# Who makes the high half of a weight tile: a cast DMA, or a copy on GpSimd

## The chip, the cores and the metric

One core of a Trainium2 chip runs the whole program. The metric is the device time of one execution in microseconds, the median of several runs. Times inside an execution come from one profiled execution, counted from the start of its span.

## What is computed

Three transformer layers on a sequence of 512 tokens of width 1024. The first two are the same layer with two sets of weights:

```
mod  = silu(c) @ ada_w + ada_b                      # six vectors of 1024
h    = rms_norm(x) * (1 + sc_m) + sh_m
proj = h @ w_in                                     # inputs of three attentions, three gates
x    = x + g_m * ((sum over NA, MLA, GQA of sigmoid(gate) * (o @ w_br)) @ w_out)
h    = rms_norm(x) * (1 + sc_f) + sh_f
x    = x + g_f * ((silu(h @ w_gate) * (h @ w_up)) @ w_down)
```

NA is a neighbourhood attention, GQA and MLA are dense ones. The third layer mixes a short convolution, a linear recurrence (RG-LRU) and an RWKV-7 recurrence in chunks, merges them with gates, and ends with an MLP of width 4096. All is float32. Each matrix product of a weight is made of three passes on TensorE over rounded numbers (type fp32r): with w = w_hi + w_lo and h = h_hi + h_lo it sums w_hi h_hi + w_hi h_lo + w_lo h_hi.

## The kernel before

**Weight stream.** All weights pass through two rings of four slots. `raw` holds tiles of 128 x 1024 float32 as they lie in HBM (512 KB; some are 128, 256, 384 or 512 columns wide). `wR` holds for each tile the high half, `wR[:, u, 0]`, which is the weight rounded to fp32r, and the low half, `wR[:, u, 1]`, which is raw minus high, rounded too. There are 468 tiles (`G_USED`), 145 for each of the first two layers. A tile of 1024 columns feeds 24 matmuls (8 steps of 128 rows, three passes each), one of 256 or 512 columns 6 or 12.

**Raw ring.** It is shared with the rows of `ada_w`: the list `RAW` mixes 96 "mod" entries with the tiles. A mod entry is not for TensorE: VectorE multiplies it with silu(c) and sums (L1428), which frees the slot (`ada_used`). 16 mod entries come first, the other 80 lie between the tiles of layer 0: one for each attention step, three for each of the 8 MLA steps, one for each pair of tiles behind them, one for each pair in the gate/up product. Layer 1 and the third layer have none. SyncE walks through `RAW` in order (L493 to L508): before entry r it waits until entry r - 4 is done with, a tile by `tile_ready` (its subtraction has ended), a mod entry by `ada_used`.

**GpSimd (POOL).** It has nothing else to do than the loop of L515 to L532. `cast(g)` (L515) waits for the raw tile and for a free slot of `wR` (`tile_used`, counted by TensorE's last matmul on a tile), and issues a DMA from `raw` to `wR[:, u, 0]` that rounds on its way (L522). The loop issues `cast(g + 1)` first (`AHEAD = 1`), then waits for `hi_ready` of tile g and subtracts (L531), which counts `tile_ready`. So the subtraction of tile g stands in the queue behind the two waits of the cast of tile g + 1.

**TensorE.** `need_tile` waits for `tile_ready`; the passes are L327 to L329. In the first two layers the dense products are cut into steps and filled between the parts of 32 attention steps: scores (L1015), turning the probabilities (L1025), times V (L1035). Steps 0 to 7 are NA, 8 to 23 GQA, 24 to 31 MLA; a step of MLA holds 12 dense steps (a gate tile with 8, a branch tile of 512 columns with 4). Behind step 31 the rest of the gates and MLA branches follows: pairs of a 1024 and a 256 column tile, 10 dense steps. Then come the output product (`mg`), gate/up and down (`act_f`).

**VectorE (DVE)** works in program order. In an MLA step it makes the maxima, the probabilities (`prob`, L1660), mod entries, and merges a branch (L1524, L1528). In the third layer, for each of 8 blocks m of 128 channels, TensorE waits at L1162 for `kkB`, which ends a chain of VectorE work: `kB` (L1835), the end of the block before (`finish`, L1852 to L1868), `vB`, four scans (L1889), `kkB`, `aB`, `kB` (L1897 to L1906). I call this stretch, where block m follows block m - 1, a change of block.

Of the kernel before, what the change touches and what calls it, by code (L numbers as in the profile page):

```python
# [22 lines left out]
NMOD = 6  # L23
EPS = 1e-6
RING = 4
AHEAD = 1


T_IN, T_MLA, T_MERGE, T_OUT, T_GU, T_DOWN = 0, 16, 20, 20 + 4 * KD, 20 + 5 * KD, 20 + 5 * KD + 2 * KF
# [137 lines left out]
G_USED = G_MLP + 64  # L167
# [49 lines left out]
RAW_AT = {what: r for r, what in enumerate(RAW)}  # L217


def ring_source(g):  # L220

    if g >= G_OUT2:
        return T_OUT2 + g - G_OUT2, 0, 1024
    if g >= G_B2:
        return MIX_SLOTS[g - G_B2]
    l, n = divmod(g, G_LAYER)
    if n >= G_OUT:
        return T_LAYER * l + T_OUT + n - G_OUT, 0, 1024
    tile, col, cols = SLOTS[n]
    return T_LAYER * l + tile, col, cols  # L230
# [101 lines left out]
def build(nc, x, c, weights, ada_b, vec1, rpb, vec2_in, vecx_in, tables1, out):  # L332
    dram_bias = nc.dram_tensor("bias_rows", (DEPTH * 4 * 15, 127), F32, kind="Internal")
    dram_toeplitz = nc.dram_tensor("bias_toeplitz", (DEPTH * 4, GRID, 15, SKEW), F32, kind="Internal")
    with ExitStack() as ctx:
        def sb(name, shape, dt=F32, into=None):
            return (into or ctx).enter_context(nc.sbuf_tensor(name, shape, dt))

        def sem(name):
            return ctx.enter_context(nc.semaphore(name))  # L340
# [6 lines left out]
        raw = sb("raw", [P, RING, 1024])  # L347
        wR = sb("wR", [P, RING, 2, 1024], F32R)
# [48 lines left out]
        passed = sem("passed")  # L397
# [42 lines left out]
        s_pad = sem("s_pad")  # L440
        s_bias = sem("s_bias")
        raw_ready = [sem(f"raw_ready{i}") for i in range(RING)]
        hi_ready = [sem(f"hi_ready{i}") for i in range(RING)]
        tile_ready = sem("tile_ready")
        tile_used = sem("tile_used")
        ada_used = sem("ada_used")
# [44 lines left out]
        @block.sync  # L491
        def _(sp):
            sp.dma_start(cs[:], c.broadcast_to([P, D])).then_inc(s_c, 16)  # L493
            for r, (what, n) in enumerate(RAW):
                if r == RING:
                    for dst, src in ((xT, x), (adab, ada_b), (vl, vec1), (tab, tables1["axial"]), (vecx, vecx_in),
                                     (tabm, tables1["rope"]), (colmask, tables1["colmask"]), (ident, tables1["ident"]),
                                     (blk, tables1["blk"])):
                        sp.dma_start(dst[:], src).then_inc(s_in, 16)
                if r >= RING:  # L500
                    before, number = RAW[r - RING]
                    if before == "mod":
                        sp.wait_ge(ada_used, number + 1)
                    else:
                        sp.wait_ge(tile_ready, number + 1)
                tile, col, cols = (n, 0, 1024) if what == "mod" else ring_source(n)
                source = weights[tile if what == "mod" else N_ADA + tile, :, col:col + cols]
                sp.dma_start(raw[:, r % RING, 0:cols], source).then_inc(raw_ready[r % RING], 16)  # L508
            sp.wait_ge(fin_ready, KD)
            sp.dma_start(out, xT[:]).then_inc(s_out, 16)  # L510
            sp.wait_ge(s_out, 16)

        @block.gpsimd
        def _(pool):

            def cast(g):
                u, cols, r = g % RING, ring_source(g)[2], RAW_AT["tile", g]
                pool.wait_ge(raw_ready[r % RING], (r // RING + 1) * 16)
                if g >= RING:
                    pool.wait_ge(tile_used, g - RING + 1)  # L520
                pool.sem_inc(passed, 1)
                pool.dma_start(wR[:, u, 0, 0:cols], raw[:, r % RING, 0:cols]).then_inc(hi_ready[u], 16)  # L522

            for g in range(AHEAD):
                cast(g)
            for g in range(G_USED):
                if g + AHEAD < G_USED:
                    cast(g + AHEAD)
                u, cols, r = g % RING, ring_source(g)[2], RAW_AT["tile", g]
                pool.wait_ge(hi_ready[u], (g // RING + 1) * 16)  # L530
                nc.gpsimd.tensor_tensor(wR[:, u, 1, 0:cols], raw[:, r % RING, 0:cols], wR[:, u, 0, 0:cols], ALU.subtract  # L531
                                        ).then_inc(tile_ready, 1)  # L532

        @block.scalar
        def _(act):
# [54 lines left out]
            for l in range(DEPTH):  # L590
# [19 lines left out]
                def turn(j):  # L610
                    _, tile, _ = TURNS[j]
                    act.wait_ge(vt_turned, 5 * l + j + 1)
                    if 32 * l + 8 * (j // 3) > 0:
                        act.wait_ge(pv_done, 32 * l + 8 * (j // 3))
                    A(vt[:, tile].rearrange("p a n -> p (a n)"), ps[:, PT + j % 2, :], ACT.Copy).then_inc(vt_copied, 1)
# [231 lines left out]
        def _(pe):  # L847
# [72 lines left out]
            for l in range(DEPTH):  # L920
# [7 lines left out]
                def dense(first, end):  # L928

                    for p in range(first, end):  # L930
                        kind, n, _, slot, last = PRODS[p]
                        t, signal = TI + slot, tile_used if last else part_ready
                        if kind == "in":
# [29 lines left out]
                def turn(j):  # L963
                    _, _, tile = TURNS[j]
                    evacuated(pe, Count(PR + {4: 0, 5: 1, 15: PIDX["in", 15], 8: PIDX["v", 0], 16: PIDX["v", 1]}[tile]))
                    before = 64 * l + {0: 0, 1: 0, 2: 8, 3: 40, 4: 40}[j]
                    if before:
                        pe.wait_ge(p_copied, before)
                    for b in range(4):
                        mm = nc.tensor.transpose(ps[:, PT + j % 2, b * P:(b + 1) * P], pj[:, tile, b * P:(b + 1) * P], ident[:])  # L970
                    mm.then_inc(vt_turned, 1)
# [1239 lines left out]
```

## Time and profile before

| | |
|---|---|
| median of 3 runs | 3166.22 us (3163.53 to 3168.85) |
| the profiled execution's own time | 3169.7 us |
| its span | 3167.9 us |
| TensorE busy | 2930.3 us, 92% |
| VectorE busy | 1698.2 us, 54% |
| GpSimd busy | 1279.5 us, 40% |
| of it: 468 subtractions, L531 | 1016.2 us |
| of it: 468 cast DMA instructions, L522 | 267.4 us |
| cast DMA traffic | 218.4 MB of 503.85 MB, 19.5% of the 16 DMA engines' time |
| mean granted clock of TensorE | 0.973 |

A row of the profile by line names the source line, the engine, the operation, what it writes and reads, its shape, how often it ran, its busy time and mean, and then how long its engine sat idle just before it and what ended that. In a timeline each row is an instruction, or several that were merged (x3): start, duration, then in brackets an idle time of that engine and what ended it. The chain of waits goes back from the last instruction, at each step to what released it. A row of VectorE can be longer than its work: time in which an instruction is held up after it has started counts as busy.

### The profile page before, as it was taken

What the parts mean: (1) busy time and instruction counts of PE and PEld (TensorE: products, weight loads), DVE (VectorE), ACT (ScalarE), POOL (GpSimd) and SP (SyncE); (2) the same over time, 40 slices, a digit from 0 to 9 for tenths busy, and PEclk for the clock granted to TensorE, in tenths of its full rate; (3) what the DMA queues carried; (4) which work ended last, traced back from release to release, by engine and by line L of the source; (5) the groups of instructions that cost most, each with busy time, mean ns of one, the idle gap of its engine ahead of it and who ended that gap; (6) DMA issues with size and microseconds to landing.
All of it is one profiled execution on the core that took longest, in us unless ns stands there. A gap on an engine that the chain in (4) does not pass through costs nothing.

```text
span 3167.9 us, 44134 instructions
## 1 busy us (share of the span) xinstructions
PE 2930.3 (92%) x18104; PEld 2265.4 (72%) x18104; DVE 1698.2 (54%) x2263; ACT 698.0 (22%) x1183; POOL 1279.5 (40%) x940
## 2 busy tenths in 40 slices
PE   2899988999998999999999969999999999999997
PEld 1666666787786767777888757777777777778786
DVE  4488775566513776445443274665465466463352
ACT  2343220200002443201000033223233323220000
POOL 1323334455564333354555522333233323345553
PEclk8899999999999999999999989999999999999999
DMA  8644556577766233364555532333233333445553
GB/s 271 180 136 141 190 200 200 178 239 236 235 218 176 93 93 122 120 199 162 193 192 197 198 109 99 106 119 121 89 125 114 112 104 117 142 159 190 182 192 113
DMA packets 174631, 503.85 MB, mean 159 GB/s; under 512 B 41206, under 2 KB 56566, under 8 KB 174198
## 3 DMA queue, kind: packets, MB, share of 16 engines
q1 hardware_dynamic: 82800, 274.75, 26.7%
q0 software_dynamic: 67392, 218.40, 19.5%
q10 hardware_dynamic: 24262, 8.21, 1.6%
q8 instruction: 127, 2.08, 0.3%
q14 instruction: 50, 0.41, 0.0%
HBM read 280.76 MB, written 6.06 MB: 91 GB/s over the span
## 4 chain that ended last, share of the span: by engine, by line
PE 78%; DVE 10%; DMA 4%; issue 3%; POOL 2%; ACT 2%; ACTq 1%; SPq 0%; DVEq 0%; POOLq 0%
PE ps L327 22%; PE ps L328 20%; PE ps L329 20%; DMA raw<-in_weights_dram 4%; PE ps L1184 3%; PE ps L1015 2%; POOL wR L531 2%; PE ps L1025 2%; PE ps L1035 2%; PE ps L1229 1%; DVE work L1465 1%; DVE dB L1889 1%; DVE kB L1901 1%; PE ps L1328 1%; DVE yB L1862 1%
## 5 line engine op out<-in xcount | busy, mean ns | idle before, releaser
L327 PE MATMUL ps<-hR,wR 128*128 128x512 f32 x2320 | 960.6, 414 | 117.2 <-DVE hR L1472 52.1
L531 POOL TENSOR_TENSOR wR<-raw,wR 128x1024 fp32r<-128x1024 f32 (+3 forms) x468 | 1016.2, 2171 | 69.9 <-DMA wR<-raw 52.4
L522 POOL DMA_DIRECT2D wR<-raw x468 | 267.4, 571 | 1783.8 <-issue 1321.8
L328 PE MATMUL ps<-hR,wR 128*128 128x512 f32 x2320 | 916.7, 395 | 0.0
L329 PE MATMUL ps<-hR,wR 128*128 128x512 f32 x2320 | 916.1, 395 | 0.0
L327 PEld LDWEIGHTS ps<-hR,wR 128*128 128x128 f32 x2320 | 443.5, 191 | 249.5 <-issue 134.0
L329 PEld LDWEIGHTS ps<-hR,wR 128*128 128x128 f32 x2320 | 442.6, 191 | 97.2
L328 PEld LDWEIGHTS ps<-hR,wR 128*128 128x128 f32 x2320 | 444.6, 192 | 86.6 <-issue 4.8
L1428 DVE CUSTOM_DVE_ANT_0 raw<-raw,cs 128x1024 f32<-128x1024 f32 x96 | 165.0, 1728 | 72.1 <-DMA raw<-in_weights_dram 65.7
L557 ACT ACTIVATE sq<-xT 128x512 f32<-128x512 f32 x56 | 35.4, 633 | 493.8 <-DVE xT L1479 341.9
L1479 DVE SCALAR_TENSOR_TENSOR xT<-ps,lm,xT 128x512 f32<-128x512 f32 x32 | 24.0, 751 | 223.1 <-PE ps L329 223.1
L327 PE MATMUL ps<-act_f,wR 128*128 128x512 f32 x352 | 140.2, 398 | 2.4 <-POOL wR L531 2.4
L329 PE MATMUL ps<-act_f,wR 128*128 128x512 f32 x352 | 139.2, 396 | 0.0
L328 PE MATMUL ps<-act_f,wR 128*128 128x512 f32 x352 | 139.2, 395 | 0.0
L694 ACT ACTIVATE tg<-ps 128x512 f32<-128x512 f32 x44 | 26.3, 599 | 438.3 <-PE ps L329 438.3
L667 ACT ACTIVATE pT<-ps 128x512 f32<-128x512 f32 x128 | 70.0, 596 | 196.8 <-PE ps L1025 196.8
L1710 DVE SCALAR_TENSOR_TENSOR work<-ps,work 128x512 f32<-128x512 f32 x44 | 30.4, 692 | 154.7 <-PE ps L329 154.7
L1015 PE MATMUL ps<-pj 64*128 64x512 f32 (+1 forms) x256 | 96.1, 652 | 16.3 <-DVE prob L1660 14.8
L2047 DVE TENSOR_TENSOR xT<-ps,xT 128x512 f32<-128x512 f32 x24 | 16.6, 692 | 158.5 <-PE ps L329 157.8
L327 PE MATMUL ps<-mlpR,wR 128*128 128x512 f32 x256 | 101.3, 396 | 0.0
L328 PE MATMUL ps<-mlpR,wR 128*128 128x512 f32 x256 | 100.9, 394 | 0.0
L329 PE MATMUL ps<-mlpR,wR 128*128 128x512 f32 x256 | 100.9, 394 | 0.0
(358 smaller groups left out, 4153.7 us busy)
## 6 DMA issues: line engine op xcount, KB each, us to landing
raw<-in_weights_dram SPq DMA_DIRECT2D x490, 512.0 KB, 3.3
wR<-raw POOLq DMA_DIRECT2D x394, 512.0 KB, 2.9
raw<-in_weights_dram SPq DMA_DIRECT2D x50, 128.0 KB, 2.9
wR<-raw POOLq DMA_DIRECT2D x50, 128.0 KB, 2.0
raw<-in_weights_dram SPq DMA_DIRECT2D x16, 256.0 KB, 3.2
wR<-raw POOLq DMA_DIRECT2D x16, 256.0 KB, 2.6
bias_toeplitz<-bias_rows ACTq DMA_DIRECT2D x8, 476.2 KB, 15.8
bias<-bias_toeplitz ACTq DMA_DIRECT2D x16, 224.0 KB, 5.7
```

The lines of the kernel that those rows point to most:

```text
L327: mm(out, w_hi, r_hi, start=first, stop=False)
L328: mm(out, w_hi, r_lo, start=False, stop=False)
L329: return mm(out, w_lo, r_hi, start=False, stop=last)
L522: pool.dma_start(wR[:, u, 0, 0:cols], raw[:, r % RING, 0:cols]).then_inc(hi_ready[u], 16)
L531: nc.gpsimd.tensor_tensor(wR[:, u, 1, 0:cols], raw[:, r % RING, 0:cols], wR[:, u, 0, 0:cols], ALU.subtract).then_inc(tile_ready, 1)
L557: A(sq[:, q.mod(2), :], src, ACT.Square).then_inc(sq_ready, 1)
L667: A(pT[:, h].rearrange("p a n -> p (a n)"), ps[:, PT + h, :], ACT.Copy).then_inc(p_copied, 1)
L1015: MM(ps[:, SC + h, :], q, k, start=True, stop=True).then_inc(scores_ready, 1)
L1025: mm = nc.tensor.transpose(ps[:, PT + h, kb * P:(kb + 1) * P], prob[:, h, kb * P:(kb + 1) * P], ident[:])
L1035: mm = MM(ps[64 * h:64 * h + 64, OB, 0:P], vt[:, tile, kb, 64 * h:64 * h + 64], pT[:, h, kb, :], start=(kb == 0), stop=(kb == 3))
L1184: return MM(ps[half_of(at_half), bank, col + 64 * cc:col + 64 * cc + 64], left[half_of(half), h, cc, :], right[half_of(half), h, cc, :], s ...
L1428: V.tensor_tensor_reduce(raw[:, r % RING, :], raw[:, r % RING, :], cs[:], 1.0, 0.0, ALU.mult, ALU.add, accum_out=mod[:, j:j + 1]).then_inc ...
```

## The change

GpSimd makes the high half itself with a `tensor_copy` from `raw` to `wR[:, u, 0]` (float32 to fp32r), waits for that on a semaphore of its own, and subtracts at once. The cast DMA, its four semaphores and the cast that ran one tile ahead are gone. The copy waits for what the cast waited for.

```
-AHEAD = 1
...
-        hi_ready = [sem(f"hi_ready{i}") for i in range(RING)]
+        hi_done = sem("hi_done")
...
         @block.gpsimd
         def _(pool):
 
-            def cast(g):
+            for g in range(G_USED):
                 u, cols, r = g % RING, ring_source(g)[2], RAW_AT["tile", g]
                 pool.wait_ge(raw_ready[r % RING], (r // RING + 1) * 16)
                 if g >= RING:
                     pool.wait_ge(tile_used, g - RING + 1)
-                pool.sem_inc(passed, 1)
-                pool.dma_start(wR[:, u, 0, 0:cols], raw[:, r % RING, 0:cols]).then_inc(hi_ready[u], 16)
-
-            for g in range(AHEAD):
-                cast(g)
-            for g in range(G_USED):
-                if g + AHEAD < G_USED:
-                    cast(g + AHEAD)
-                u, cols, r = g % RING, ring_source(g)[2], RAW_AT["tile", g]
-                pool.wait_ge(hi_ready[u], (g // RING + 1) * 16)
+                nc.gpsimd.tensor_copy(wR[:, u, 0, 0:cols], raw[:, r % RING, 0:cols]).then_inc(hi_done, 1)
+                pool.wait_ge(hi_done, g + 1)
                 nc.gpsimd.tensor_tensor(wR[:, u, 1, 0:cols], raw[:, r % RING, 0:cols], wR[:, u, 0, 0:cols], ALU.subtract
                                         ).then_inc(tile_ready, 1)
```

GpSimd's queue at the start of the program, before (DMA is the cast of a tile, TENSOR_TENSOR its subtraction, in brackets what it waits for):

```order
L522 DMA wR<-raw 128x1024 [waits raw_ready1]
L522 DMA wR<-raw 128x1024 [waits raw_ready0]
L531 ISA
L531 TENSOR_TENSOR wR<-raw,wR 128x1024 [waits hi_ready0]
L522 DMA wR<-raw 128x1024 [waits raw_ready2]
```

and now (CAST is the copy):

```order
L520 CAST wR<-raw 128x1024 [waits raw_ready1]
L522 ISA
L522 TENSOR_TENSOR wR<-raw,wR 128x1024 [waits hi_done]
L520 CAST wR<-raw 128x1024 [waits raw_ready0]
L522 TENSOR_TENSOR wR<-raw,wR 128x1024 [waits hi_done]
```

The subtraction of tile 0 no longer stands behind the wait for the raw tile 1.

The same queue in the MLA steps of layer 0, tiles 39 (1024 columns), 40 (512) and 41 (1024), before:

```order
L522 DMA wR<-raw 128x512 [waits raw_ready0,tile_used]
L531 TENSOR_TENSOR wR<-raw,wR 128x1024 [waits hi_ready3]
L522 DMA wR<-raw 128x1024 [waits raw_ready3,tile_used]
L531 TENSOR_TENSOR wR<-raw,wR 128x512 [waits hi_ready0]
L522 DMA wR<-raw 128x512 [waits raw_ready1,tile_used]
L531 TENSOR_TENSOR wR<-raw,wR 128x1024 [waits hi_ready1]
```

and now:

```order
L520 CAST wR<-raw 128x1024 [waits tile_used,raw_ready3]
L522 TENSOR_TENSOR wR<-raw,wR 128x1024 [waits hi_done]
L520 CAST wR<-raw 128x512 [waits tile_used,raw_ready0]
L522 TENSOR_TENSOR wR<-raw,wR 128x512 [waits hi_done]
L520 CAST wR<-raw 128x1024 [waits tile_used,raw_ready3]
L522 TENSOR_TENSOR wR<-raw,wR 128x1024 [waits hi_done]
```

Each subtraction now follows the copy of its own tile, and waits for the raw data and the slot of no later tile.

## Rows read from the trace of the kernel before

**Rows 1.** The page, the chain that ended last: shares of the span by engine, by line.
```profile
PE 78%; DVE 10%; DMA 4%; issue 3%; POOL 2%; ACT 2%; ACTq 1%; SPq 0%; DVEq 0%; POOLq 0%
PE ps L327 22%; PE ps L328 20%; PE ps L329 20%; DMA raw<-in_weights_dram 4%; PE ps L1184 3%; PE ps L1015 2%; POOL wR L531 2%; PE ps L1025 2%; PE ps L1035 2%; PE ps L1229 1%; DVE work L1465 1%; DVE dB L1889 1%; DVE kB L1901 1%; PE ps L1328 1%; DVE yB L1862 1%
```

**Rows 2.** Busy time by stretches; behind the engines: granted clock, DMA share, GB/s.
```profile
119.20:342.90 223.70, 215.34 (x1235) 151.23 (x1236) 178.75 (x376) 95.66 (x194) 69.43 (x62) 0.98 0.44 147
...
367.25:446.20 78.95, 65.78 (x322) 47.07 (x321) 61.22 (x91) 16.69 (x36) 24.30 (x20) 0.96 0.59 200
1235.20:1320.00 84.80, 84.80 (x449) 63.80 (x448) 47.20 (x83) 23.22 (x49) 34.04 (x29) 1.00 0.39 130
446.20:542.40 96.20, 78.64 (x328) 59.73 (x328) 57.38 (x75) 9.44 (x18) 39.88 (x37) 0.91 0.60 193
1320.00:1397.30 77.30, 71.03 (x329) 55.12 (x328) 34.35 (x46) 9.28 (x17) 36.64 (x35) 1.00 0.52 157
...
2100.00:2210.00 110.00, 105.50 (x1059) 81.12 (x1058) 63.94 (x78) 34.24 (x52) 36.58 (x27) 1.00 0.34 116
```

**Rows 3.** Timeline of TensorE, scores of MLA steps 26, 27 and 31, layer 0.
```profile
367.25 1.98 PE L1015 MATMUL ps<-pj 96*128 96x512 f32 x4
383.58 1.66 PE L1015 MATMUL ps<-pj 96*128 96x512 f32 x3 [2.53 <-DVE prob L1660]
...
446.18 3.65 PE L1015 MATMUL ps<-pj 96*128 96x512 f32 x4 [2.51 <-DVE prob L1660]
```

**Rows 4.** The chain that ended last, MLA steps of layer 0: start, us, what.
```profile
380.51 4.53 DMA raw<-in_weights_dram
...
385.62 0.57 POOL wR L522
...
386.22 1.29 POOL wR L531
...
387.90 3.91 DMA raw<-in_weights_dram
```

**Rows 5.** Timeline of GpSimd behind the last attention step of layer 1.
```profile
1350.32 0.57 POOL L522 DMA_DIRECT2D wR<-raw  x1
1354.45 2.38 POOL L531 TENSOR_TENSOR wR<-raw,wR 128x1024 fp32r<-128x1024 f32 x1 [3.56 <-DMA wR<-raw]
...
1362.43 2.37 POOL L531 TENSOR_TENSOR wR<-raw,wR 128x1024 fp32r<-128x1024 f32 x1 [3.80 <-DMA wR<-raw]
```

**Rows 6.** By line, GpSimd alone, shapes kept apart.
```profile
L531 POOL TENSOR_TENSOR wR<-raw,wR 128x1024 fp32r<-128x1024 f32 x394 | 950.2, 2412 | 65.0 <-DMA wR<-raw 48.9 <-PE ps L329 8.0
...
L531 POOL TENSOR_TENSOR wR<-raw,wR 128x512 fp32r<-128x512 f32 x16 | 20.9, 1303 | 0.3
...
L2201 POOL MEMSET const-float32-0.0<- 128x1 f32 x1 | 0.1, 99 | 0.2 <-issue 0.2
```

**Rows 7.** Timeline of VectorE at a change of block of the third layer.
```profile
2085.08 3.10 DVE L1835 SCALAR_TENSOR_TENSOR kB<-shf,vec,kB 128x512 f32<-128x512 f32 x1 [8.34 <-ACT kB L743]
...
2091.00 2.27 DVE L1862 SCALAR_TENSOR_TENSOR yB<-sg,yB 128x512 f32<-128x512 f32 x1
2093.30 0.69 DVE L1864 TENSOR_TENSOR msum<-msum,yB 128x512 f32<-128x512 f32 x1
2094.03 2.73 DVE L1866 TENSOR_SCALAR mR<-msum 128x512 fp32r<-128x512 f32 x1
...
2098.53 3.69 DVE L1889 TENSOR_TENSOR_SCAN dB<-ones,e 128x128 f32<-128x128 f32 x3
...
2105.05 3.05 DVE L1901 TENSOR_TENSOR kB<-kB,work 128x512 f32<-128x512 f32 x1
```

**Rows 8.** Timeline of GpSimd at the same change of block, two of ten rows.
```profile
2093.46 0.57 POOL L522 DMA_DIRECT2D wR<-raw  x1 [0.73 <-issue]
2094.05 2.41 POOL L531 TENSOR_TENSOR wR<-raw,wR 128x1024 fp32r<-128x1024 f32 x1
```

**Rows 9.** Timeline of TensorE where that change of block ends.
```profile
2109.60 1.10 PE L1162 MATMUL ps<-kkB,aB 64*64 64x64 f32 x46 [2.43 <-DVE kkB L1906]
```

## The prediction

> **What bounds the kernel now.** I read first the chain that ended last [rows 1]: 78% of the span is TensorE, so the only time to win or lose is where TensorE stands still. Two other entries bear on the change: GpSimd's subtraction and the raw weight DMA are 6% together, VectorE 10%. So there are places where the weight stream sets the pace, and others where VectorE does. The view by stretches finds the first kind [rows 2]. The MLA steps 27 to 31 of layer 0 take 78.95 us (367.25 to 446.20), 15.8 each, with TensorE busy for 65.78. The seven steps of layer 1 at 1235.20 take 84.80, 12.1 each, with TensorE never idle. Behind the last step the rest of gates and branches takes 96.20 us in layer 0 and 77.30 in layer 1, for the same matmuls.
>
> The chain in those MLA steps names the cause [rows 4]: raw DMA 4.53, cast instruction 0.57, subtraction 1.29, raw DMA 3.91, and so on with no TensorE in it. The reader should see that the subtraction at 386.22 is that of tile 40, while the raw DMA and the cast before it are those of tile 41. The subtraction of tile g stands behind the landing of raw tile g + 1, and the raw ring gives a slot back only after a subtraction. So each tile costs one raw DMA, one cast and one subtraction in a row, 15.4 us for two tiles, and VectorE and then TensorE (waits of 2.5 us for `prob` [rows 3]) follow that pace. In layer 1 behind the steps it is the cast DMA itself: issued at 1350.32, and the subtraction starts at 1354.45, 4.13 later; the 1024 column subtractions are 8.0 apart [rows 5], while 10 dense steps of three passes, at the 12.1 us of an MLA step less its attention part, need about 7.
>
> The second kind of place is the change of block in the third layer. TensorE waits 2.43 us for `kkB` [rows 9], and VectorE in front of it works without a pause from 2085.08. Five of its rows are long [rows 7]: 3.10, 2.27, 2.73, 3.69 (three scans) and 3.05, where a two-input instruction of the same width takes 0.69 (2093.30). Each of them ends about 0.3 to 0.5 us after a subtraction on GpSimd has ended: 2094.03 + 2.73 = 2096.76, against 2094.05 + 2.41 = 2096.46 [rows 8]. VectorE is held up by GpSimd. The five rows sum to 14.8 us; their own work I estimate as 4 x 0.7 plus 1.3 for the scans, so 10.7 us are lost, 2.1 for each tile.
>
> **Removed: cast DMA, cast-ahead.** In the MLA steps of layer 0 the loop becomes: raw DMA about 4.6, copy, subtraction 2.4, with one tile out of two in it, because tile g + 1 is no longer in front of tile g. That is some 9 us for a step of two tiles, below the 12.1 that TensorE needs. At 12.1 the five steps would take 60.6, a gain of 18.3. I take 15: VectorE is busy for 61.22 us there [rows 2], 12.2 a step, part of it held up, and will not quite keep 12.1. Behind the steps, layer 0 should come down to the present pace of layer 1, 96.2 - 77.3 = 18.9; I take 18. In layer 1 seven pairs go from 8.0 to 7.0: 7. **Gain: 15 + 18 + 7 = 40 us** (bounds 20 and 50: half of the loop replaced by another wait; or layer 0 reaching layer 1's new pace). The traffic of the casts (19.5% of the DMA engines) was beside other work and is costed at nothing. At the start of the program the last mod entry lands up to 5 us earlier, since tile 0 is subtracted earlier, but the subtractions of tiles 2 and 3 then meet the first norm on VectorE; nothing is taken. The 267 us of cast instructions go from a GpSimd that is 60% idle: nothing, too.
>
> **Added: a copy of each tile.** No row shows one on GpSimd. Its bounds are a one-element instruction, 0.10 us, and the subtraction, 2.41 for 1024 columns. The subtraction costs (2412 - 1303) / 512 = 2.17 ns a column over a fixed 0.19 [rows 6], for two inputs. A copy has one; with half the slope it takes 0.19 + 1.11 = **1.3 us**, which I take. GpSimd then needs about 3.8 us for a tile of 1024 columns. TensorE needs 12.1 us for 12 dense steps and attention, so above 5 for such a tile: GpSimd doesn't become the bound.
>
> The price is on VectorE. A change of block has five tiles. Before, GpSimd kept VectorE out for 2.4 us per tile, and left it alone during the cast instruction. Now it is 1.3 + 0.1 + 2.4. That is 1.4 more for each, 7.0 for five; the first copy is over when `kB` starts, and once VectorE has an instruction that reads PSUM: 7.0 - 1.3 - 1.1 = 4.6 us. TensorE's work up to L1162 is fixed and it waits already, so all of it is TensorE's wait. Seven such changes, and half a one at the end: **34 us**. The granted clock follows: over 367 to 446 it was 0.96 with 13.2 us idle [rows 2], 3.2 us lost, or 0.24 for each idle us, where a whole block of the third layer now has 4.5 idle at 1.00. 34 x 0.24 = **8 us**. In the NA and GQA steps of layer 0 VectorE is busy for 178.75 of 223.7 us, with 31 tiles (62 GpSimd instructions); in both layers some 62 copies of 0.9 on average are 56 us of closed time, and if an eighth becomes TensorE's wait, **7 us**. Sum of the losses 49 (bounds 0 and 110: no hold-up by copies; copies of 2.4 us, which make it 10 a change).
>
> The Trainium skill, "SBUF — State Buffer", section "Who interferes with whom", says that a VectorE instruction with two SBUF inputs contends with a GpSimd instruction that reads SBUF, and that the second one is blocked to the end. By that rule the copy closes the port as the subtraction does, and the loss stands; rows 7 and 8 agree for the subtraction, and no row shows it for a copy.
>
> **Sum.** 3169.7 - 40 + 49 = 3178.7 against the profiled execution, whose time is 3.5 us above the median of the runs. So 3175 against 3166.2, slower by 0.3%. A difference of 0.2%, 6 us, is about what a measurement can tell from none.
>
> **Rivals.**
> 1. *VectorE's chain hardly lengthens* (faster): it gets its turn between copy and subtraction, or a copy doesn't keep it out. For it: every long row ends with a subtraction, none is known for a copy. Against: it is a GpSimd instruction that reads and writes the same buffers. Then 40 of gain stay and 0 to 20 are lost: 3126 to 3148. It decides below about 2 us a change of block.
> 2. *A shorter copy* (no change). At 1.1 us the extra closed time is 1.2 a tile, 3.7 a change, 28 in all, clock 6, attention 6: 3166.2 - 40 + 40 = 3166. The rows leave room for it, since half the slope is only a guess between 0.1 and 2.4.
> 3. *A slow copy* (slower): like the subtraction, 2.4 us. Ten us for each change, 75, with clock 18 and attention 15, gain reduced to 30: about 3244.
>
> On the second: the Trainium skill, "GPSIMD Engine Reference", section "Elementwise — side-by-side cycle accounting", gives 1.03 cycles of 1.2 GHz per element for simple one-input bodies and 2.6 for a two-input one. The rows agree with its 2.6 (2.17 ns). By its 1.03 the copy would be an estimated 1.1 us, and the sum that of this rival.
>
> **Chances.** The forecast's mechanism 0.38 (3168 to 3190 for itself; 0.28 of it slower, 0.10 same), rival 1 0.27, rival 2 0.27 (0.15 same, 0.08 faster, 0.04 slower), rival 3 0.08. That makes faster 0.35, same 0.25, slower 0.40. The range leaves out rival 3 and the lower part of rival 1: 3135 to 3205.
>
> **What would show it.** In the profile after: MLA steps 27 to 31 of layer 0 at 12.1 to 12.7 us each, and no chain of raw DMA and subtraction there; the rest behind them near 77 and 70 us. A row for the copy with its mean; at 1.3 the first step of the loss holds. At a change of block, long VectorE rows of about 3.5 us or twice as many of them, and `kkB` waits of some 7 us instead of 2.43 (seven of them). The prediction is wrong in its sign if those waits stay under 5 us while layer 0's stretches shrink as said, and wrong in its gain if MLA steps still take over 14 us with VectorE waiting for a mod entry.

## The result, and the profile after

| | kernel before | changed kernel |
|---|---|---|
| median of the runs, first set | 3165.71 us (4 runs) | 3088.86 us (3084.45 to 3090.34, 4 runs) |
| median of the runs, second set | 3164.79 us (9 runs) | 3086.49 us (3085.41 to 3090.01, 5 runs) |
| the profiled execution | 3169.7 us | 3084.45 us |
| its span | 3167.9 us | 3082.7 us |
| DMA traffic | 503.85 MB | 285.45 MB |

The change makes the kernel faster: ratio 0.9751, interval 0.9736 to 0.9767, and 0.9755 (0.9742 to 0.9768) in the second set. The forecast was 3175 us with a range of 3135 to 3205. Time and sign are both wrong.

The page of the changed kernel, busy time and then the chain that ended last (before: [rows 1]):

```profile
PE 2904.9 (94%) x18104; PEld 2255.3 (73%) x18104; DVE 1718.3 (56%) x2263; ACT 699.2 (23%) x1183; POOL 1533.4 (50%) x940
...
PE 84%; DVE 9%; issue 3%; ACT 2%; DMA 1%; ACTq 0%; POOL 0%; DVEq 0%; POOLq 0%
```

TensorE's share of the chain went from 78% to 84%, the DMAs' from 4% to 1%, GpSimd's from 2% to nothing. Of the 85.2 us between the two spans, TensorE stood idle for 59.8 less (237.6 before, 177.8 now) and was busy for 25.4 less with the same 18104 matmuls, at a mean granted clock of 0.982 instead of 0.973.

The changed kernel by stretches (columns as in [rows 2]): NA and GQA steps of layer 0, its MLA steps 24 to 31, the rest behind them, that rest in layer 1, and the third layer from the first matmul that takes `kkB` to the end of the blocks ("the mixing stage" below):

```profile
110.00:325.70 215.70, 210.42 (x1235) 148.28 (x1236) 173.49 (x376) 95.83 (x194) 80.24 (x62) 1.00 0.31 104
325.70:410.60 84.90, 84.90 (x450) 63.86 (x449) 75.65 (x127) 23.81 (x49) 48.28 (x29) 1.00 0.56 193
410.60:480.60 70.00, 69.36 (x330) 55.68 (x329) 53.32 (x63) 9.28 (x17) 51.36 (x35) 1.00 0.50 164
1247.90:1317.10 69.20, 69.20 (x330) 55.79 (x329) 40.40 (x44) 9.27 (x17) 45.23 (x36) 1.00 0.30 95
1809.50:2650.50 841.00, 812.93 (x8297) 624.25 (x8296) 486.62 (x592) 259.60 (x396) 322.53 (x198) 0.99 0.17 57
```

Second to fourth row: TensorE is never idle, or for 0.64 us, where it stood still for 17.6 of 96.20 us behind the steps of layer 0. The last row, for the kernel before:

```profile
1890.40:2734.30 843.90, 810.15 (x8297) 622.45 (x8296) 473.39 (x592) 258.75 (x396) 267.88 (x199) 0.99 0.33 111
```

The stage where I had expected 42 us of loss is 2.9 us shorter: VectorE is busy for 13 us more in it, TensorE for 2.8 us more, and TensorE stands idle for 5.7 us less.

GpSimd's copies by line, 1024 columns (columns as in [rows 6]); then its timeline in an MLA step of layer 0:

```profile
L520 POOL CAST wR<-raw 128x1024 fp32r<-128x1024 f32 x394 | 441.4, 1120 | 1243.4 <-PE ps L328 1138.9 <-DMA raw<-in_weights_dram 104.4
...
371.68 1.44 POOL L520 CAST wR<-raw 128x1024 fp32r<-128x1024 f32 x1 [4.99 <-PE ps L328]
373.19 3.22 POOL L522 TENSOR_TENSOR wR<-raw,wR 128x1024 fp32r<-128x1024 f32 x1
376.36 1.07 POOL L520 CAST wR<-raw 128x512 fp32r<-128x512 f32 x1
377.52 1.30 POOL L522 TENSOR_TENSOR wR<-raw,wR 128x512 fp32r<-128x512 f32 x1
```

Of GpSimd's idle time in front of a copy, 1139 us end with TensorE giving a slot back and 104 with a raw tile landing. In the MLA step it waits 4.99 us for TensorE: the weight stream is now ahead, and the chain of [rows 4] is gone.

TensorE's waits over the whole program, before and then after (us in total, times, longest):

```profile
PE ps L327 <- POOL wR L531: 25.3, 18, 3.4
...
PE ps L1162 <- DVE kkB L1906: 17.1, 7, 2.5
PE ps L1015 <- DVE prob L1660: 14.8, 10, 2.9
...
PE ps L327 <- ACT gB L743: 0.9, 2, 0.6
```

```profile
PE ps L326 <- ACT gB L734: 7.3, 7, 1.3
...
PE ps L326 <- POOL wR L522: 4.0, 2, 3.0
PE ps L1153 <- DVE kkB L1897: 3.2, 7, 0.6
...
PE ps L1006 <- DVE prob L1651: 2.8, 4, 1.3
```

Waits for a weight tile fell from 25.3 to 4.0 us. Those for `prob` fell from 14.8 to 2.8 us, and none is left in the MLA steps. The wait for `kkB`, whose length was to decide the sign, fell from 2.5 to at most 0.6 us each. The waits for `gB` grew from 0.9 to 7.3 us. Of the waits not shown here, that for `pj` changed most, from 20.6 to 11.3 us.

Stage lengths in one profile each, from TensorE's timeline. "L0" is layer 0, "L0 rest behind" the gates and branches behind its MLA steps, "out to scores" its output product, gate/up, down and the entry of layer 1, "L1 attention" all 32 steps of layer 1 with the rest behind them, "to kkB" what lies between the attention of layer 1 and the mixing stage:

| us | start | L0 NA, GQA | L0 MLA | L0 rest behind | L0 out to scores | L1 attention | to kkB | mixing | end |
|---|---|---|---|---|---|---|---|---|---|
| before | 119.2 | 223.7 | 103.3 | 96.2 | 480.8 | 374.1 | 493.1 | 843.9 | 433.6 |
| changed | 110.0 | 215.7 | 84.9 | 70.0 | 472.8 | 363.7 | 492.4 | 841.0 | 432.2 |
| changed, again | 111.0 | 215.7 | 84.9 | 70.1 | 475.2 | 363.7 | 493.4 | 838.3 | 431.9 |
| copy one tile ahead | 115.1 | 216.1 | 104.3 | 84.7 | 474.8 | 364.2 | 499.0 | 850.4 | 431.2 |
| cast DMA, not ahead | 119.3 | 221.0 | 100.3 | 119.1 | 666.4 | 399.8 | 682.1 | 812.7 | 579.9 |
| slot one tile later | 108.4 | 219.4 | 84.9 | 70.4 | 477.6 | 364.9 | 498.8 | 857.2 | 431.3 |
| copy twice | 114.2 | 220.6 | 84.9 | 76.8 | 472.1 | 365.6 | 498.0 | 869.8 | 431.4 |
| memset before the copy | 111.9 | 214.4 | 84.9 | 70.5 | 473.2 | 364.8 | 495.5 | 857.2 | 431.2 |
| spare DMA for each tile | 118.2 | 220.8 | 84.9 | 72.8 | 474.9 | 366.6 | 500.8 | 848.2 | 436.1 |
| spare DMA, 8 tiles | 117.4 | 215.6 | 84.9 | 70.1 | 472.0 | 365.3 | 494.2 | 835.4 | 431.7 |
| no copy | 113.8 | 215.4 | 84.9 | 69.7 | 473.0 | 363.0 | 493.7 | 815.0 | 432.0 |
| no copy, slot later | 107.9 | 213.9 | 84.9 | 70.4 | 469.5 | 363.4 | 493.5 | 832.6 | 431.5 |
| cast DMA in mixing only | 114.8 | 215.6 | 84.9 | 70.1 | 475.4 | 363.7 | 492.5 | 817.7 | 432.1 |
| the same, again | 115.5 | 215.6 | 84.9 | 70.0 | 473.4 | 365.3 | 490.8 | 812.3 | 431.3 |

With the same code in a stage, profiles differ by up to 6 us in the mixing stage (841.0 and 838.3, with the eight spare DMAs 835.4; 817.7 and 812.3), and by up to 5.5 at the start (110.0, 111.0, 114.8, 115.5). Smaller differences there are read from medians of runs, or not at all.

### The profile page after: what moved, and what is told of

It reads as the page before. It is cut to its first block, busy times and chain, and to the rows that moved or that the text cites. A ratio compares the mean times of both kernels' runs of the same rounds, so it can differ in the third digit from the quotient of the medians.

```text
span 3082.7 us, 44130 instructions
## 1 busy us (share of the span) xinstructions
PE 2904.9 (94%) x18104; PEld 2255.3 (73%) x18104; DVE 1718.3 (56%) x2263; ACT 699.2 (23%) x1183; POOL 1533.4 (50%) x940
## 2 busy tenths in 40 slices
DMA packets 107239, 285.45 MB, mean 93 GB/s; under 512 B 33718, under 2 KB 41654, under 8 KB 106806
## 3 DMA queue, kind: packets, MB, share of 16 engines
q1 hardware_dynamic: 82800, 274.75, 26.3%
## 4 chain that ended last, share of the span: by engine, by line
PE 84%; DVE 9%; issue 3%; ACT 2%; DMA 1%; ACTq 0%; POOL 0%; DVEq 0%; POOLq 0%
PE ps L326 24%; PE ps L328 22%; PE ps L327 22%; PE ps L1175 3%; PE ps L1006 3%; PE ps L1016 2%; PE ps L1026 2%; DMA raw<-in_weights_dram 1%; PE ps L1220 1%; DVE mg L1524 1%; PE ps L1319 1%; PE ps L1153 1%; DVE mR L1857 1%; PE ps L1321 1%; DVE work L1456 1%
## 5 line engine op out<-in xcount | busy, mean ns | idle before, releaser
L520 POOL CAST wR<-raw 128x1024 fp32r<-128x1024 f32 (+3 forms) x468 | 487.5, 1042 | 1474.4 <-PE ps L328 1369.9
L522 POOL TENSOR_TENSOR wR<-raw,wR 128x1024 fp32r<-128x1024 f32 (+3 forms) x468 | 1051.0, 2246 | 37.4
L1419 DVE CUSTOM_DVE_ANT_0 raw<-raw,cs 128x1024 f32<-128x1024 f32 x96 | 164.6, 1731 | 24.0 <-DMA raw<-in_weights_dram 16.2
L685 ACT ACTIVATE tg<-ps 128x512 f32<-128x512 f32 x44 | 26.5, 602 | 431.9 <-PE ps L328 431.9
L1448 DVE TENSOR_TENSOR act_f<-work,act_f 128x512 fp32r<-128x512 f32 x44 | 103.3, 2348 | 1.5
```

The source lines that it names most:

```text
L520: nc.gpsimd.tensor_copy(wR[:, u, 0, 0:cols], raw[:, r % RING, 0:cols]).then_inc(hi_done, 1)
L1419: V.tensor_tensor_reduce(raw[:, r % RING, :], raw[:, r % RING, :], cs[:], 1.0, 0.0, ALU.mult, ALU.add, accum_out=mod[:, j:j + 1]).then_inc ...
L1448: V.tensor_tensor(lo, full, hi, ALU.subtract).then_inc(signal, n)
```

## The experiments

My theory after the result: the gain is the order (a subtraction that stands behind no other tile), the copies do cost what a closed port costs, and something I had left out pays for them. The rivals: the copies cost nothing; or it is the cast DMA's traffic and instruction that were dear.

**The order alone, with a copy (e1).** The copy of tile g + 1 stands ahead of the subtraction of tile g, as the cast did:

```
+            copy_hi(0)
+            for g in range(G_USED):
+                if g + 1 < G_USED:
+                    copy_hi(g + 1)
```

> The copy stays, the order goes back: copy of tile g + 1 ahead of the subtraction of tile g. Theory A (order: the gain is that a subtraction no longer stands behind the landing of the next raw tile): most of the gain of 77 us is lost, MLA steps 27 to 31 of layer 0 are 14 to 15 us again, time 3130 to 3155. Rival B (latency: the gain is the cast DMA's 3 to 4 us between its issue and the subtraction): the time stays near the changed kernel's, 3085 to 3100, MLA steps at 12.1.

Measured: 3140.88 us, ratio 0.9924 (0.9907 to 0.994). Some 24 us below the kernel before, 52 above the changed one. The chain in the MLA steps of layer 0 of this kernel (start, us, what):

```profile
351.30 4.13 DMA raw<-in_weights_dram
...
356.48 2.27 POOL wR L528
...
359.15 5.34 DMA raw<-in_weights_dram
...
365.69 2.38 POOL wR L528
```

It is [rows 4] with a copy of 1.0 us where the cast was: the landing of raw tile g + 1, then the subtraction of tile g, which frees the slot for the next raw DMA. The stretch takes 104.3 us against 103.3 before and 84.9 in the changed kernel. So in the old order, taking the cast DMA away does nothing for it. Nor does the new order alone do it: with the cast DMA (e2 below) the stretch takes 100.3. The gain needs both. In e6 below, where the subtraction no longer stands behind the landing of the next raw tile but still comes as late as that tile's slot, the stretch takes 84.9: it was the landing.

This run is also the closest test of the forecast loss, for it has copies at the old places. In the mixing stage (850.4 us) TensorE waits:

```profile
PE ps L1159 <- DVE kkB L1903: 15.7, 7, 2.3
...
PE ps L326 <- ACT gB L740: 7.0, 7, 1.2
```

The stage is 6.5 us longer than before and not 42, VectorE is busy for 14 us more, and the waits for `kkB` have not grown at all (17.1 before). Those for `gB` have, by 6.1 us, and those for `rB` by 2.1.

**The cast DMA, right ahead of its own subtraction (e2).** The kernel before with one number changed:

```
-AHEAD = 1
+AHEAD = 0
```

> The kernel before with only the order changed: the cast DMA of tile g directly ahead of its own subtraction. Theory A: most of the gain comes, 3095 to 3120, since the raw ring no longer waits for the next tile; each tile then costs GpSimd about 0.6 + 3.5 + 2.4 = 6.5 us in a row, so where tiles of 1024 columns follow each other at 5.5 us the stream itself becomes the bound. Then the pure product stretches grow by about 1 us a tile, some 200 tiles, and the time is above 3250. Rival B: no gain in the MLA steps of layer 0 (15 us), and the same loss in the product stretches.

Measured: 3700.26 us, ratio 1.1688 (1.1668 to 1.1707). Its GpSimd behind the MLA steps of layer 1, where tiles of 1024 and 256 columns alternate:

```profile
1598.18 2.41 POOL L531 TENSOR_TENSOR wR<-raw,wR 128x1024 fp32r<-128x1024 f32 x1 [3.40 <-DMA wR<-raw]
1600.54 0.57 POOL L522 DMA_DIRECT2D wR<-raw  x1
1604.59 0.73 POOL L531 TENSOR_TENSOR wR<-raw,wR 128x256 fp32r<-128x256 f32 x1 [3.48 <-DMA wR<-raw]
...
1610.83 2.33 POOL L531 TENSOR_TENSOR wR<-raw,wR 128x1024 fp32r<-128x1024 f32 x1 [4.78 <-DMA wR<-raw]
```

A pair takes 12.65 us (1598.18 to 1610.83), of which GpSimd stands 8.26 (3.48 + 4.78) in front of a landing. The good order is to be had only with a high half that comes at once; the cast ran ahead for a reason. One stage went the other way: mixing fell from 843.9 to 812.7. That was not expected by anything I had written, and led to e8.

**A slot later by one tile (e6).** The changed kernel's own order, but the copy of tile g waits for the slot that before the cast of g + 1 waited for. In the kernel before the subtraction of g stood behind that wait:

```
-                if g >= RING:
-                    pool.wait_ge(tile_used, g - RING + 1)
+                if g >= RING - 1:
+                    pool.wait_ge(tile_used, g - RING + 2)
```

> The changed kernel, but the copy of tile g waits until tile g - 3 has been used, not g - 4: the subtraction comes at the same tile of TensorE as in the kernel before, and stands behind no later tile. Theory A: the time stays at 3085 to 3095. Rival C (depth: the gain is that low halves are now made one tile earlier): it goes back by a third or more of the gain, 3115 or above.

Measured: 3114.18 us, ratio 0.9837 (0.9819 to 0.9855), 25 us over the changed kernel, 16 of them in the mixing stage. TensorE's waits there:

```profile
PE ps L1153 <- DVE kkB L1897: 19.8, 7, 2.8
PE ps L326 <- ACT rB L734: 12.6, 7, 1.8
PE ps L326 <- ACT gB L734: 7.4, 7, 1.4
```

The waits for `kkB` are back near their old size (17.1) and the others are as in the changed kernel. GpSimd in the last part of a change of block shows why: here a tile of 1024 columns is converted where `kkB` is made (its next `aB` row starts at 2039.61), in the changed kernel one of 256. First this kernel, then the changed one:

```profile
2033.43 2.72 POOL L522 TENSOR_TENSOR wR<-raw,wR 128x1024 fp32r<-128x1024 f32 x1
2039.06 1.28 POOL L520 CAST wR<-raw 128x1024 fp32r<-128x1024 f32 x1 [2.90 <-PE ps L328]
2040.42 2.69 POOL L522 TENSOR_TENSOR wR<-raw,wR 128x1024 fp32r<-128x1024 f32 x1
```

```profile
2007.49 2.72 POOL L522 TENSOR_TENSOR wR<-raw,wR 128x1024 fp32r<-128x1024 f32 x1
2010.14 1.51 POOL L520 CAST wR<-raw 128x1024 fp32r<-128x1024 f32 x1
2011.74 2.72 POOL L522 TENSOR_TENSOR wR<-raw,wR 128x1024 fp32r<-128x1024 f32 x1
2015.36 1.04 POOL L520 CAST wR<-raw 128x1024 fp32r<-128x1024 f32 x1 [0.90 <-PE ps L328]
2016.47 2.72 POOL L522 TENSOR_TENSOR wR<-raw,wR 128x1024 fp32r<-128x1024 f32 x1
2022.08 0.65 POOL L520 CAST wR<-raw 128x256 fp32r<-128x256 f32 x1 [2.89 <-PE ps L328]
2022.81 1.10 POOL L522 TENSOR_TENSOR wR<-raw,wR 128x256 fp32r<-128x256 f32 x1
```

The whole pattern has moved by one tile against TensorE's and VectorE's work. Before, five subtractions of 1024 columns fell between the start of `kB` and the end of `kkB` ([rows 8] has one of them); here too there are five, in the changed kernel four and one of 256.

**The copy twice (e3).** This prices a copy by adding one:

```
+                for n in range(2):
+                    nc.gpsimd.tensor_copy(wR[:, u, 0, 0:cols], raw[:, r % RING, 0:cols]).then_inc(hi_done, 1)
+                    pool.wait_ge(hi_done, 2 * g + n + 1)
```

> The changed kernel with each copy made twice (1.04 us more of GpSimd for each 1024 column tile, same output). If copies keep VectorE out as a subtraction does, the waits for kkB at the changes of block grow from 0.5 us to 2 to 4 us each and the time by 15 to 40 us. If VectorE gets its turns between the instructions, or a copy doesn't keep it out, the time grows by less than 10 us.

Measured: 3136.54 us, ratio 0.991 (0.989 to 0.993). One of its four runs took 7272 us, for a reason that is not known; the median of the other three, which lie within 2 us, is 3135.96. That is 47.1 us over the changed kernel. The mixing stage is 28.8 us longer, and VectorE is busy for 537.26 us in it instead of 486.62. TensorE waits there for `gB` 21.6 us in place of 7.3 and for `rw_off` 10.3 us, for which it did not wait. The waits for `kkB`, which I had expected to grow to 2 to 4 us each, stay at 0.8 or less (3.7 in all). A copy is not free, but its price doesn't fall where I had put it.

**No copy (e7).** From tile 4 on, only one column is copied. The kernel leaves out the rest of the high halves, so it gives a time and no usable result:

```
-                nc.gpsimd.tensor_copy(wR[:, u, 0, 0:cols], raw[:, r % RING, 0:cols]).then_inc(hi_done, 1)
+                part = cols if g < RING else 1
+                nc.gpsimd.tensor_copy(wR[:, u, 0, 0:part], raw[:, r % RING, 0:part]).then_inc(hi_done, 1)
```

> The changed kernel with one column copied instead of the tile from tile 4 on: it leaves out the high halves, all waits and the rest of the stream stay. The difference to the changed kernel is the price of the copies. If they cost by keeping VectorE out: 10 to 30 us less between the first kkB and the last product of the third layer (841 there now), 3055 to 3080 in all. If they are free behind the shift of one tile: within 5 us.

Measured: 3059.17 us, ratio 0.9653 (0.9632 to 0.9674): 29.7 us below the changed kernel. In the mixing stage:

```profile
1813.40:2628.40 815.00, 804.59 (x8296) 619.25 (x8296) 443.61 (x592) 258.85 (x396) 241.04 (x198) 1.00 0.18 58
```

and TensorE's waits in it:

```profile
PE ps L1154 <- DVE kkB L1898: 3.4, 7, 0.5
PE ps L326 <- ACT rB L735: 2.4, 7, 0.5
```

26.0 us less than 841.00, of which 17.7 are TensorE's idle time (28.07 to 10.41) and 8.3 its busy time, at a clock of 1.00 instead of 0.99. VectorE is busy for 43 us less. So copies hold VectorE as the prediction said, and the mixing stage pays for it. But it pays elsewhere: what goes with the copies are the waits for `rB` (12.8 to 2.4 us) and `gB` (7.3 to none), while those for `kkB` stay as they are (3.2 and 3.4). This price was there all along; something else had made up for it.

**No copy, and the slot one tile later (e9).** Both edits together:

> As the run without copies, and also one tile later. With this one, the run one tile later, the run without copies and the changed kernel the two effects in the third layer come apart: by the runs so far 16 us for one tile later with copies. If the shift matters by which tiles' conversions fall into the change of block, it stays at 10 to 20 us without copies; if it matters only through the copies' hold, it falls under 5.

Measured: 3074.49 us, ratio 0.971 (0.9691 to 0.9728), mixing 832.6. Depth, that is, the slot of tile g and not that of g + 1, is worth 17.6 us of the mixing stage without copies (815.0 to 832.6) and 16.2 with them (841.0 to 857.2). The waits for `kkB` grow with the slot's delay in both pairs, from 3.4 to 14.7 us and from 3.2 to 19.8. So in this stage depth is worth something without any copy. Over the whole program the medians say 15 us without copies and 25 with them, so that the two effects simply add up isn't shown there. At the late slot and with no copies the stage is still 11.3 us shorter than in the kernel before, which has the cast DMA, its instruction and the old order. The difference lies in the waits for `rB` (10.9 before, 2.5 here) and `kkB` (17.1, 14.7).

**A memset before the copy (e4).** It writes the place of the low half and reads nothing:

```
+                nc.gpsimd.memset(wR[:, u, 1, 0:cols].bitcast(F32), 0.0).then_inc(hi_done, 1)
```

> The changed kernel with a memset of the low half's place ahead of each copy: GpSimd work of the order of a copy that writes SBUF and reads nothing (same output). If reading is what keeps VectorE out, VectorE's rows at a change of block stay as in the changed kernel and the time moves by less than 5 us; if any GpSimd instruction keeps it out, it grows as with the doubled copy.

Measured: 3107.76 us, ratio 0.9816 (0.9798 to 0.9834), 19 over the changed kernel; mixing 857.2. GpSimd and then VectorE of this kernel at a change of block:

```profile
2015.48 0.95 POOL L520 MEMSET wR<- 128x1024 f32 x1 [0.71 <-PE ps L328]
2016.38 1.48 POOL L521 CAST wR<-raw 128x1024 fp32r<-128x1024 f32 x1
2017.94 2.74 POOL L523 TENSOR_TENSOR wR<-raw,wR 128x1024 fp32r<-128x1024 f32 x1
```

```profile
2015.48 0.75 DVE L1847 SCALAR_TENSOR_TENSOR yB<-yB,vec,bnB 128x512 f32<-128x512 f32 x1 [0.16 <-DVE yB L1844]
...
2018.44 2.78 DVE L1856 TENSOR_TENSOR msum<-msum,yB 128x512 f32<-128x512 f32 x1
```

During the memset a two-input row of VectorE takes 0.75, its plain length; during the subtraction another takes 2.78. In the whole stage 28 rows of VectorE lie inside a memset of 0.95 us, and all of them have their plain length. So the memset holds nobody, but it puts copy and subtraction 0.95 us later. That this lateness is what costs the 19 us is an inference: VectorE is busy for 506.16 us in the stage instead of 486.62, and the waits that grow are those for `rB` (12.8 to 25.6), not those for `kkB` (3.2 to 0.3). I had expected less than 5 us. If it is the lateness, up to 19 of the 47 us that e3 adds can be lateness rather than closed time, and e7 has the same reserve the other way, since its subtractions also come some 0.8 us earlier. The price of a copy holds both.

**A spare DMA for each tile (e5), and for the first eight (e10).** As many bytes as the casts moved, from HBM to HBM and not from SBUF to SBUF, issued by GpSimd between copy and subtraction:

```
+                if g >= 8:
+                    pool.wait_ge(s_dummy[g % 8], g // 8 * 16)
+                pool.dma_start(dram_dummy.ap()[g % 8, :, 0:cols], weights[N_ADA + ring_source(g)[0], :, 0:cols]).then_inc(s_dummy[g % 8], 16)
```

> The changed kernel with a DMA of the tile's size for each tile, from the weights in HBM to a spare place in HBM, issued on GpSimd's queue and waited for by no one (8 in flight at most): the traffic and the issue of the cast come back, its waits do not. Rival D (traffic: the removed 218 MB slowed raw DMAs and the bias DMAs at the start): the stretch up to the first scores goes from 110 back to about 119 us, the MLA steps of layer 0 go above 13 us, time 3110 or more. If traffic was beside other work: 3085 to 3100, mostly from the start.

Measured: 3125.11 us, ratio 0.9865 (0.9845 to 0.9884): 36 over the changed kernel, spread over every stage but the MLA steps (8.2 at the start, 5.1 in the NA and GQA steps, 8.4 to `kkB`, 7.2 mixing, 3.9 at the end). So one DMA instruction of 0.53 us ahead of each subtraction and one more stream of DMA are worth tens of us in this kernel, not nothing. Which of the two it is, how much of it is that the subtraction comes later (as in e4), and how near this traffic is to the cast's, it does not tell.

> The changed kernel with spare DMAs of 512 KB for the first 8 tiles alone. If the start (first scores at 110 us against 119 before and 118 with traffic throughout) is won by the removed traffic beside the bias DMAs: first scores at 115 to 118, 3094 to 3098 in all. If it is won by the order of the conversions: within 2 us of the changed kernel.

Measured: 3091.05 us, ratio 0.9761 (0.9743 to 0.9778). The profile has the start at 117.4 us, but the median is only 2 us over one set of the changed kernel's runs and 5 over the other, inside the interval. Inconclusive: the start's 9.2 us of gain stay unexplained in their parts, and with 110.0 to 115.5 us for the same code (e8 and e12 included) their size is uncertain, too.

**The cast DMA in the mixing stage only (e8).** Copy elsewhere; there, the cast DMA directly ahead of its own subtraction, as in e2:

```
+                if G_B2 + 2 <= g < G_OUT2:
+                    casts[u] += 16
+                    pool.dma_start(wR[:, u, 0, 0:cols], raw[:, r % RING, 0:cols]).then_inc(hi_ready[u], 16)
+                    pool.wait_ge(hi_ready[u], casts[u])
```

> A hybrid: the changed kernel, but for the tiles of the third layer's mixing stage (98 tiles between its first pair and the output product) the high half comes from the cast DMA, issued directly ahead of its own subtraction. In the all-DMA run of that order this stage took 812.7 us against 841.0 now, since GpSimd needs some 6.6 us a tile and so keeps VectorE out for a smaller share of a change of block. Expected: 810 to 820 there, 3055 to 3070 in all, faster than both kernels. If the stage's gain came from what stood around it in that run: no change from 3089.

Measured: 3059.89 us, ratio 0.966 (0.9642 to 0.9677). GpSimd at the same change of block:

```profile
2001.62 0.57 POOL L524 DMA_DIRECT2D wR<-raw  x1 [3.58 <-PE ps L328]
2004.61 2.39 POOL L530 TENSOR_TENSOR wR<-raw,wR 128x1024 fp32r<-128x1024 f32 x1 [2.43 <-DMA wR<-raw]
...
2012.54 2.36 POOL L530 TENSOR_TENSOR wR<-raw,wR 128x1024 fp32r<-128x1024 f32 x1 [4.92 <-DMA wR<-raw]
...
2018.80 2.52 POOL L530 TENSOR_TENSOR wR<-raw,wR 128x1024 fp32r<-128x1024 f32 x1 [3.37 <-DMA wR<-raw]
```

Each subtraction waits for its own cast, so they come 7.9 and 6.3 us apart, and only the last two shown meet VectorE's chain. From the start of `kB` to the end of the last `kkB` it takes 18.7 us (2007.89 to 2026.57), against 23.8 in the changed kernel (2002.13 to 2025.91) and 24.5 before (2085.08 to 2109.54). The stage has the casts' traffic and their instructions again (DMA share 0.37, before 0.33) and is as short as with no copies.

**Both once more, on one chip (e11, e12).** The changed kernel and e8, unchanged, in five rounds:

> The changed kernel once more, beside the hybrid on one chip: 3085 to 3092, and what its stages vary by between two profiles (so far 841.0 and, with the same code there, 835.4 us in the mixing stage).

> The hybrid (cast DMA in the mixing stage alone) once more: 3055 to 3068, 20 to 30 us below the changed kernel, all of it in the mixing stage. If the difference on one chip is under 10 us, the earlier one came from the chip.

Measured: 3086.49 us, ratio 0.9755 (0.9742 to 0.9768), and 3060.91 us, ratio 0.9673 (0.9658 to 0.9688). The mixed form beats both kernels, by 26 us the changed one, and the whole of it lies in the mixing stage (812.3 against 838.3 us in the profiles).

## Why the prediction was wrong

**The split of the gain, by medians.** Copy for cast DMA in the old order: 24 us (e1). The subtraction no longer behind the next raw tile's landing: 27 (e1 to e6). No longer behind the next tile's slot: 25 (e6 to the changed kernel). The three are steps in this sequence, not prices that hold in any other.

**The gains, 40 us.** Right in mechanism and small in size. The MLA steps went to 12.1 us each, 84.9 for seven: 18.4, the full difference, for which 15 was taken since VectorE was thought too busy. The rest behind them gave 26.2 instead of 18. I had expected layer 0 to come down to the old pace of layer 1 (77.3), but it came to the new one (70.0 and 69.2), which the bound of 50 had in it. In layer 1 the rest gave 8.1 against 7.

**The loss, 49 us: the step that failed.** "A change of block has five tiles", 4.6 us more each time, "all of it is TensorE's wait" for `kkB`, 34 in all, clock 8. That copies hold VectorE was right: taking them away gives 26.0 us in that stage, of which 8.3 with the clock. The size and the place were wrong. With copies at the old places (e1) the stage is 6.5 us longer and not 42, and the seven waits for `kkB` sum to 15.7 us where they had 17.1. With the late slot and the new order (e6) they sum to 19.8, 0.4 more each and not 4.6. VectorE's timeline shows it, too. From the start of `kB` to the end of the last `kkB` the seven changes of block take:

| | us |
|---|---|
| kernel before | 24.2 to 25.0 |
| copy one tile ahead (e1) | 25.4 to 25.7 |
| slot one tile later (e6) | 26.0 to 26.3 |
| the same without copies (e9) | 22.5 to 22.7 |
| changed kernel | 23.8 to 24.1 |
| no copy (e7) | 20.9 to 21.1 |

Copies in place of casts lengthen the chain by some 1 us at the old places. Two premises failed. A copy does not close VectorE out for its whole length (last section). And TensorE's work up to L1162 is not fixed in time: it waits for `rB` and `gB` on the way, and it is there that copies cost it time (e1, e7).

At a copy of 1.3 us I had priced this loss at 42; the copy takes 1.04 us alone and 1.12 on average. Beside it the Trainium skill, "GPSIMD Engine Reference", section "Elementwise — side-by-side cycle accounting", gave an estimated 1.1 us: trace and rule agree, and I should have gone by it rather than by half the slope of [rows 6]. But that alone leads to rival 2, no change. Two terms were missing besides:

- *Depth*, costed at nothing. By [rows 4] I saw that the subtraction leaves its place behind tile g + 1, and used it only where the weight stream was late. In the mixing stage it isn't late, and the same move takes a conversion of 1024 columns out of the chain before `kkB` and puts one of 256 there. That is worth 16.2 us there with copies (e6) and 17.6 without (e9).
- *The cast DMA*, "costed at nothing" in traffic and instruction. The kernel before stands 11.3 us above e9 in the mixing stage. What costs that stays open: the instruction of 0.57 us ahead of every subtraction, the traffic, or the old order, which e9 doesn't have either; e5 does not separate them. That traffic and instruction cost it wherever they stand is unlikely, since e8 has both and takes 812.3 to 817.7 us, where e7 has neither and takes 815.0.

Together: 843.9 - 11.3 - 17.6 + 26.0 = 841.0. That it closes is no proof, since the terms are the differences of four profiles in a row (843.9, 832.6, 815.0, 841.0); each is known to some 5 us. Another way through the runs gives other terms: + 6.5 for copies in the old order (e1), + 6.8 for the move away from the landing (e6), - 16.2 for the slot.

**NA and GQA, 7 us of loss.** The measured change is a gain, 8.0 us in layer 0 and 2.4 in layer 1. e1 has most of it (7.6 of 8.0) with the same number of copies and the old order, and e2, which has the new order and the casts, has 2.7. So here it is mostly the cast that went. My "eighth of the closed time" had no row behind it.

**Not in the sum.** 9.2 us at the start, 8.0 between the output product of layer 0 and the first scores of layer 1, and 2.1 elsewhere. For the start I had named the earlier mod entry and then set its gain to nothing against a held-up norm. There a pair of VectorE's rows of the norm (L1456, L1465 before) took 4.21 us where it took 6.30, the opposite.

In one line: 9 us of loss were forecast on the profiled execution and 85 of gain came; 12.7 are in the gains' sizes, 45 in the mixing stage, 17 in the attention steps, 19 in stages left out, within a rounding of 0.4. Among the rivals, the first (faster, VectorE's chain hardly lengthens) had the direction and what decides it, a `kkB` wait under 5 us. It had half of the reason: VectorE does get a turn between copy and subtraction. But copies count all the same (26.0 us in e7), and the chain is no longer than before because it lost one large conversion. And its 3126 was still 37 us too high, since the gain was taken too small.

Three small slips of the prediction change nothing above: its first rival's upper end is 3146 (3166 - 40 + 20) and not 3148; the five long rows end 0.3 to 0.6 us after a subtraction, not 0.3 to 0.5; and by its own rate of 0.24 rival 2's clock term is 6.7 us and not 6.

## What to carry to other kernels

When an edit takes an instruction out from behind a wait of the next item, everything on that queue moves by one item, also where the queue isn't late: lay the new positions against the critical chain of each stage, and look for which sizes now fall on it. An engine that competes for a port is priced by what lies in the critical window, not by its sum, and slowing it down there on purpose (a DMA that spaces its instructions) can be worth more than making it quick. A DMA that "hides beside other work" still has an issuing instruction and a latency in an in-order queue: one run without it is the price, while a dummy in its place (e5) brings costs of its own.

## What the runs showed of the hardware

- A float32 to fp32r copy on GpSimd takes 1.04 us for 128x1024 when nobody interferes, and 0.40 for 128x256 (2012.41 in e6), that is 0.83 ns a column over some 0.2 us, where the two-input subtraction has 2.17 [rows 6].
- The hold goes both ways. VectorE gets its turn between a copy and the subtraction behind it, and then GpSimd's row is the long one. A piece of the changed kernel, VectorE, beside GpSimd's rows from 2007.49 above:

```profile
2008.48 2.27 DVE L1853 SCALAR_TENSOR_TENSOR yB<-sg,yB 128x512 f32<-128x512 f32 x1
2010.79 1.41 DVE L1855 TENSOR_TENSOR msum<-msum,yB 128x512 f32<-128x512 f32 x1
2012.23 2.51 DVE L1857 TENSOR_SCALAR mR<-msum 128x512 fp32r<-128x512 f32 x1
```

  The `msum` row of 1.41 us is 0.7 of waiting for the copy and 0.7 of work, and in the same time the copy lasts 1.51 and the subtraction 2.72 instead of 1.04 and 2.4. So this copy costs VectorE 0.7 us there and not its whole length, and it costs GpSimd, too. The Trainium skill, "SBUF — State Buffer", section "Who interferes with whom", has the second instruction blocked to the end of the first; the rows agree, for the copy as well, and add that a pair of GpSimd instructions is not one block.
- A memset on GpSimd, which only writes, holds no row of VectorE: in the mixing stage of e4, 28 rows lie inside one, and each takes its plain length, the 14 two-input ones of 512 columns 0.75 us.
